# First piece of w_in from columns of x without their norm, the divisor applied to its results

## The reference

```
h = x * rsqrt(mean(x * x) + EPS) * g_mix          # per token, then per feature
z = h @ w_in + b_in
glu_a, glu_b, q, k, v, gates = parts of z
u = glu_a * sigmoid(glu_b); u = causal conv over 31 tokens with conv_w, ...
```

## Time and profile before

| what | value |
|---|---|
| median of 3 runs | 1159.46 us (1158.85 to 1159.47) |
| the profiled execution | 1159.07 us, its span 1157.2 us |
| TensorE busy | 1115.2 us, 96% |
| DVE / ACT / POOL busy | 29% / 15% / 6% |
| DMA | 441.69 MB, mean 382 GB/s |
| chain that ended last | PE 90%, DMA 6% |

### The profile page before, as it was taken

The page is one execution under the profiler, slowest core; times in us unless marked ns, Lnnn a source line. Parts: engine busy times, 40 slices in busy tenths (PEclk is TensorE's granted clock), DMA queues, the critical chain, the costliest instruction groups (busy, mean ns, idle before and its releaser), DMA issues.

```text
span 1157.2 us, 13576 instructions
## 1 busy us (share of the span) xinstructions
PE 1115.2 (96%) x5299; PEld 524.6 (45%) x5299; DVE 333.2 (29%) x795; ACT 177.7 (15%) x351; POOL 68.4 (6%) x67
## 2 busy tenths in 40 slices
PE   8999999999999999999999999999999999999997
PEld 7888888853333333333333333333333333333332
DVE  2999973553111111111111111111111111111111
ACT  2111375231000000010011001000000000000012
POOL 2350013330000000000000000000000000000000
PEclk9999999999999999999999999999999999999999
DMA  9975443689999999999999999999999999999996
GB/s 284 348 238 159 146 168 142 264 361 396 422 427 428 434 432 432 432 428 432 432 434 433 432 430 432 432 433 434 432 430 429 433 434 434 432 429 430 433 426 264
DMA packets 55462, 441.69 MB, mean 382 GB/s; under 512 B 4231, under 2 KB 34185, under 8 KB 38792
## 3 DMA queue, kind: packets, MB, share of 16 engines
q1 hardware_dynamic: 53616, 439.89, 91.6%
q0 software_dynamic: 432, 0.95, 0.4%
q10 hardware_dynamic: 1384, 0.44, 0.2%
HBM read 440.08 MB, written 1.05 MB: 381 GB/s over the span
## 4 chain that ended last, share of the span: by engine, by line
PE 90%; DMA 6%; another core or an unknown queue 2%; DVE 1%; ACT 0%; issue 0%; ACTq 0%; SPq 0%; DVEq 0%
PE bank L1570 55%; PE bank L1310 16%; PE bank L1535 5%; DMA arena<-in_w_up 4%; PE bank L1520 4%; PE bank L1426 2%; PE bank L1606 2%; PE bank L1577 1%; DMA conv_w_rows_then_biases<-in_conv_w 1%; PE bank L1527 1%; PE bank L1613 1%; PE bank L1457 1%; PE bank L1333 1%; PE bank L1358 0%; DMA arena<-in_x 0%
## 5 line engine op out<-in xcount | busy, mean ns | idle before, releaser
L1570 PE MATMUL bank<-arena,columns_x_block_scatter 128*64 128x512 f32 x3004 | 672.6, 595 | 28.6 <-DMA arena<-in_w_up 19.7
L1570 PEld LDWEIGHTS bank<-arena,columns_x_block_scatter 128*64 128x64 f32 x3004 | 220.2, 137 | 433.9 <-issue 413.8
L1310 PE MATMUL bank<-arena 128*128 128x256 f32 x928 | 203.7, 380 | 1.0 <-DVE arena L876 1.0
L1310 PEld LDWEIGHTS bank<-arena 128*128 128x128 f32 x928 | 175.2, 190 | 26.6 <-issue 2.7
L909 DVE SCALAR_TENSOR_TENSOR arena<-arena x240 | 96.4, 477 | 0.1
L1150 DVE TENSOR_SCALAR bias_selector<-ones_bf,expert_onehot 96x64 bf16<-96x64 bf16 x32 | 7.6, 236 | 267.9 <-PE bank L1527 267.9
L1185 DVE TENSOR_SCALAR gate_clipped<-bank 128x512 f32<-128x512 f32 x32 | 22.1, 692 | 205.8 <-PE bank L1570 205.8
L1189 DVE TENSOR_SCALAR hidden<-bank 128x512 f32<-128x512 f32 x32 | 22.2, 692 | 182.8 <-PE bank L1570 182.8
L1535 PE MATMUL bank<-y_block,columns_x_block_scatter 64*128 64x512 f32 x248 | 61.5, 614 | 0.0
L794 ACT ACTIVATE columns_x_block_scatter<-gate_clipped 128x512 f32<-128x512 f32 x32 | 20.1, 630 | 241.2 <-DVE gate_clipped L1185 241.2
L1520 PE MATMUL bank<-x_normed,select 128*64 128x512 f32 x240 | 56.8, 592 | 0.0
(11 more groups left out here) (209 smaller groups left out, 503.9 us busy)
## 6 DMA issues: line engine op xcount, KB each, us to landing
arena<-in_w_up SPq DMA_DIRECT2D x25, 4096.0 KB, 44.1
arena<-in_w_down SPq DMA_DIRECT2D x25, 4096.0 KB, 45.3
arena<-in_w_gate SPq DMA_DIRECT2D x24, 4096.0 KB, 42.9
arena<-in_w_in SPq DMA_DIRECT2D x20, 1024.0 KB, 12.0
arena<-in_w_gate SPq DMA_DIRECT2D x9, 2048.0 KB, 16.2
arena<-in_w_up SPq DMA_DIRECT2D x9, 2048.0 KB, 16.5
arena<-in_w_down SPq DMA_DIRECT2D x8, 2048.0 KB, 21.0
arena<-in_w_down SPq DMA_DIRECT2D x11, 1024.0 KB, 10.2
```

The source lines that it names most:

```text
L1310: last = pe.matmul(bank[n % 3][:, j * T:(j + 1) * T], w[:, c, j * P:(j + 1) * P], src[:, c, :], start=(c == 0), stop=(c == C - 1))
L1570: last = pe.matmul(dst[h * CAP:(h + 1) * CAP, :], lhs(row), cols(weights, h), start=(row == 0), stop=(row == MROWS - 1))
```

## The change

The first piece is multiplied with x's columns times g_mix only (`gainT`, which takes the room of `work`), since a token's divisor can be applied to the results of the product. For that DVE makes `gainT` ahead of `rstd_row`; TensorE starts piece 0 with it, computes the two rows between the two halves of the piece, and DVE then makes `hT` from `gainT` and `rstd_row` for all other pieces. When piece 0 is done, DVE multiplies its results with `rstd_row` into `u`, and ScalarE adds the bias in place there. The count of `vecs_out` goes up to 3, and piece 1 waits for all of `hT`.

```diff
+        gainT = work[:].rearrange("p (c t) -> p c t", c=C)
...
-            act.wait_ge(vecs_out, 2)
+            act.wait_ge(vecs_out, 3)
             act.dma_start(wrt, t_in["w_router"].rearrange("(c p) e -> p c e", p=P)).then_inc(wrt_loaded, 16)
...
-                    last = act.activation(dst[j], bank[n % 3][:, j * T:(j + 1) * T], func,
+                    last = act.activation(dst[j], dst[j] if n == 0 else bank[n % 3][:, j * T:(j + 1) * T], func,
                                           bias=vec("b_in", IN_COLS[n] // P + j))
...
-            for t in range(TT):
+            def rstd_diagonal(t):
                 dv.wait_ge(stds, t + 1)
                 step(dv.reciprocal(rstd[:, 0, t:t + 1], std[:, 0, t:t + 1]))
                 dv.tensor_scalar(diag[:, t, :], ident[:], rstd[:, 0, t:t + 1], None, ALU.mult).then_inc(diag_ready, 1)
-                if t == 0:
-                    dv.wait_ge(gmixT, 1)
-                    dv.tensor_copy(vecs[:, 0:C], bank[1][:, 0:C]).then_inc(vecs_out, 1)
-
 
             g0 = VEC["g_mix"][0]
+            rstd_diagonal(0)
+            dv.wait_ge(gmixT, 1)
+            dv.tensor_copy(vecs[:, 0:C], bank[1][:, 0:C]).then_inc(vecs_out, 1)
             dv.wait_ge(vecs_out, 1)
-            dv.wait_ge(row_out, TT)
             for c in range(C):
                 if c % (C // 2) == 0:
                     dv.wait_ge(xTp, 2 + c // (C // 2))
-                dv.scalar_tensor_tensor(hT[:, c, :], bank[3 + c // 2][:, c % 2 * T:(c % 2 + 1) * T],
-                                        vecs[:, g0 + c:g0 + c + 1], rstd_row, ALU.mult, ALU.mult).then_inc(hT_ready, 1)
+                dv.tensor_scalar(gainT[:, c, :], bank[3 + c // 2][:, c % 2 * T:(c % 2 + 1) * T],
+                                 vecs[:, g0 + c:g0 + c + 1], None, ALU.mult).then_inc(hT_ready, 1)
+            rstd_diagonal(1)
+            dv.wait_ge(hT_ready, C)
+            dv.wait_ge(row_out, TT)
+            for c in range(C):
+                dv.tensor_tensor(hT[:, c, :], gainT[:, c, :], rstd_row, ALU.mult).then_inc(hT_ready, 1)
+            dv.wait_ge(piece_done, 1)
+            dv.wait_ge(u_zero, 1)
+            for j in range(2):
+                last = dv.tensor_tensor(u[:, j, KTAPS - 1:], bank[0][:, j * T:(j + 1) * T], rstd_row, ALU.mult)
+            last.then_inc(vecs_out, 1)
...
             x_columns(1, range(C // 2, C))
-            rstd_to_row(0)
-            rstd_to_row(1)
...
-            project(0, hT, ready=hT_ready, ready_by=1)
+            project(0, gainT, (0,), ready=hT_ready, ready_by=1)
+            rstd_to_row(0)
+            rstd_to_row(1)
+            project(0, gainT, (1,))
             pe.wait_ge(vecs_loaded, 16 * (len(VEC) - 1))
             pe.wait_ge(vecs_out, 1)
             pe.transpose(bank[6][:, 0:VROWS], vrows, ident[0:VROWS, 0:VROWS]).then_inc(vecsT, 1)
+            pe.wait_ge(hT_ready, 2 * C)
             project(1, hT)
```

More of the change, by code:

```diff
@@ L887, in _ @@
             step(dv.tensor_scalar(sinks8, sinks, 1.0 / SCALE, None, ALU.mult))
-            dv.wait_ge(vecs_out, 2)
+            dv.wait_ge(vecs_out, 3)
             for h in range(NH):
@@ L1380, in _ @@
             pe.wait_ge(z_out, GATE0)
-            pe.wait_ge(vecs_out, 2)
+            pe.wait_ge(vecs_out, 3)
             for t in range(TT):
```

## The result

The changed kernel takes 1164.01 us (median of 7 runs, 1163.36 to 1164.89) where the kernel before takes 1159.46 (7 runs): a ratio of 1.0041, 95% interval 1.0032 to 1.0050. It is 4.55 us slower; 4.27 were forecast. The profiled execution took 1164.89 us, the slowest of the seven, with a span of 1163.0, 5.8 more than before. One execution, in the variant with early issues and the split fetch, took 6621.74 us for a reason that is not known, and stands outside every median and ratio given here.

What follows compares the result with a forecast made beforehand. TensorE bounds the front, the expert-weight stream the last part, so piece 2's start sets the end: +4.27 us on the path, 0 from the earlier start, 0 from additions, giving 1163.3 (1163.7 from the median); range 1161.5 to 1166.0.

Steps and rivals of the forecast that it cites:

- That nothing absorbs a delay of piece 2: From 24.39 us to the end: whatever moves piece 2's start should move the kernel's end by the same amount.
- TensorE's steps: At the start: piece 0 from 8.3 us, row matmuls between its halves, done at 15.9, 0.5 us ahead without other waits.
- The late issues: ScalarE's queue: row copies wait behind half of piece 0, so all eight DMA issues move 4.27 us later, the first to 12.66.
- The time to landing taken as it was: conv_w's DMA: 12.60 us from issue to landing kept unchanged, so issued at 15.41 it lands at 28.0.
- The rival of a queue that answers faster: ScalarE's DMA queue: first packets come sooner, conv_w lands at 25.5, shift 1.8 us, 1161.3 us; chance 0.09.
- The stop for the vector rows: Behind piece 0: TensorE stopped from 15.9 until about 19.9, a new wait of 4.0 us.
- Piece 1 behind it (7.09) ends at 27.1: After the wait for the vector rows: piece 1 takes its old 7.09 us and ends at 27.1.
- the second wait: Between pieces 1 and 2: TensorE, done with piece 1 at 27.1, waits 0.9 us for conv_w at 28.0.
- the second rival: TensorE's clock falls in the wait behind piece 0; piece 1 loses 1.7 us, 0.9 covered: shift 5.1, 1164.5 us; chance 0.15.
- the forecast: Piece 2 starts 4.27 us later, at 28.7, and so does the end; holds for shifts 3.4 to 5; chance 0.68.
- Faster than before: conv_w still lands by 23.7 and vector rows before 15.9, so TensorE's gain comes through: 1158.7 us; chance 0.04.

Runs made afterwards that it cites:

- early issues and the split fetch: Changed kernel with ScalarE's eight DMAs issued ahead of its two row copies and conv_w fetched by two DMAs (16 and 15 rows): 1158.43 us, ratio 0.9988.
- early issues: Changed kernel with ScalarE's eight DMAs issued ahead of its two row copies: 1158.65 us, ratio 0.9995.
- row matmuls first: Changed kernel with both row matmuls ahead of piece 0 on TensorE and the second diagonal ahead of the gains on DVE: 1160.01 us, ratio 0.9999.
- filled wait with the split: Changed kernel with eight unused matmuls behind piece 0 and conv_w fetched by two DMAs (16 and 15 rows): 1162.82 us, ratio 1.0024.
- late issues alone: Kernel before with one added wait, so ScalarE issues its vector-row and conv_w DMAs only after DVE made ident4, at about 12.3 us: 1163.32 us, ratio 1.0038.
- filled wait: Changed kernel with eight matmuls of 256 columns, results unused, added behind piece 0: 1164.00 us, ratio 1.0038.

## Why the prediction was right, and where not

**That nothing absorbs a delay of piece 2**: right. Among the ten profiled executions that show neither a low clock in piece 2 nor the new wait for the layer norm, the time less the start of piece 2 lies between 1133.7 (early issues) and 1135.4 (row matmuls first). Part of this spread is a low clock later on: the three highest, 1135.1 to 1135.4 (row matmuls first, early issues with the split, filled wait with the split), are the three that have one at 280 to 290 us, where the kernel before kept 1.00. With the row matmuls first:

```profile
280.00:285.00 5.00, 4.80 (x16) 1.54 (x18) 0.38 (x2) 0.43 (x2) 0.00 (x0) 0.66 1.03 428
```

**TensorE's steps**: right. Piece 0 started at 8.09 (8.3), the first half ended at 11.64 (11.87), the second at 15.7 (15.9). The first chunks' landing, not the gains, set the start in the profiled execution. The eight products for hT took 2.77 us (3.2), the two for u 0.76, both beside other waits: with early issues or the row matmuls first they cost nothing that can be measured.

**The late issues**: right, 12.29 for 12.66, a shift of 3.90 where 4.27 was worked out; 0.21 of the rest is piece 0's earlier start. The late issues alone cost 3.8 us in the kernel before, early issues give everything back, and the row matmuls ahead of piece 0 do so too. That is shown, not argued.

**The time to landing taken as it was**: right. 12.60 us became 12.66 in the changed kernel and 12.68, 12.71, 12.95 and 12.96 in the four variants where conv_w ended a wait. The rival of a queue that answers faster is out: in the changed kernel ScalarE's queue, with its first issue at 12.29, moved no packet up to 16.2, 3.9 us. The Trainium skill's 0.6 us to the first byte ("DMA: Bandwidth & Descriptors", Specifications), which stood beside that rival, is not what this trace shows beside the w_in stream.

**The stop for the vector rows**: 3.9 us (4.0).

**The step that failed is "Piece 1 behind it (7.09) ends at 27.1".** It took 9.63 us and ended at about 29.4, since the clock fell in the stop; the second wait, 0.9 us for conv_w, did not occur. So the profiled execution went by the second rival, which had a chance of 0.15, and not by the forecast, which had 0.68: piece 2 moved by 5.61 us, and the forecast held for 3.4 to 5. The rival's price was too low: 1.7 us of loss where 2.54 were lost. Its cover of 0.9 was right, so that 1.65 stood beyond conv_w's landing in place of 0.8.

The Trainium skill ("TensorE: Matmul & The Clock Gate", Part 1) has the rule that stood beside this rival, that an idle array falls to half rate and returns after work. The granted clock agrees with it at the waits of 3.9 and 5.1 us. Its fall with a wait of only 1.04 us, told below, is one that the rule, as the prediction tells it, does not foretell.

The time came out near the forecast all the same, 4.55 us by the medians for 4.27, and that is in part luck. The profiled pair is 5.82 us apart, 1.55 more than the 4.27: the clock added 1.65 and the issues, earlier than worked out, took 0.37 off. This pair is an execution 0.4 under the median of the kernel before and the slowest of the changed kernel's seven, 0.9 above its median. How much of the 4.55 us is the clock's is not shown. In the seven executions of the changed kernel the mean granted clock was 0.994 to 0.997 and in the five with the filled wait 0.995 to 0.998, which suggests that most of the seven had the low clock; yet the medians, 1164.01 and 1164.00, are the same, with a spread of about 1 us from run to run.

**Faster than before** needed conv_w to land where it did; it did not. Its price, 0.8 us, agrees with early issues, where piece 2 starts 0.75 us before 24.39 and the medians stand 0.8 apart, though the interval includes no change.

## What to carry to other kernels

When work on one engine is moved behind other work, list everything that stands behind its consumer in that consumer's program, DMA issues above all: here two small copies on ScalarE were wanted late, and eight transfers, the last of them with 12.6 us to landing, were queued behind them. Issue transfers ahead of anything that waits for computation, and see first what the issues themselves (3.0 us for the eight) hold up. A stop of TensorE can cost more than its length: behind those of 3.9 and 5.1 us the low clock took 2.5 and 1.6 more. And where two causes end close to each other, removing only one shows little.

## What was not expected of the hardware

The clock also fell where no long wait stood ahead of it: with late issues in the kernel before, piece 0 began behind transposes and 1.04 us of waiting, and its stretches show

```profile
9.00:10.00 1.00, 0.64 (x2) 0.58 (x3) 1.00 (x4) 0.00 (x0) 0.28 (x1) 0.73 1.08 366
10.00:11.00 1.00, 1.00 (x4) 0.81 (x3) 1.00 (x3) 0.00 (x0) 0.00 (x0) 0.50 1.10 357
```

with 8.83 us for piece 0. The kernel before had the same wait and order there and kept its clock in its profiled execution (7.14 us). So the same start can run either way, by 1.7 us, and this may be part of the spread from run to run. Of the 58 executions of the kernel before that ran beside the variants, the 21 with a mean granted clock of 0.998 or more have a median of 1159.3 us and the 28 with 0.996 or less one of 1159.9; where in them the clock was low is not on record.

conv_w's 31 rows went in a train of some four packets of 4 KB a us, and the same bytes in 16 and 15 rows were through in about one us, from 19.3 to 20.2, with the vector rows in four. The Trainium skill ("DMA: Bandwidth & Descriptors", Why a DMA increments its semaphore by 16 and not by 1) says that the number of rows decides how many DMA engines a copy is spread over, and by its rule a prime number above 16 leaves one. The rates of both shapes agree with that.
